# Twelve of sixteen pairs of attention probabilities turned by VectorE blocks and a round trip through HBM instead of by TensorE

## The reference, cut to what matters

```
s = einsum('bnqhgd,bnkhd->bhgnqk', qc, kb) * HEAD_DIM ** -0.5
s = where(valid, s, -1e30)
m = maximum(max(s, -1), sink)
p = exp(s - m)
denom = sum(p, -1) + exp(sink - m)
o = einsum('bhgnqk,bnkhd->bnqhgd', p / denom, vb)
```

## Time and profile before

| what | value |
|---|---|
| time, median of 3 runs | 1270.37 us (1270.3 to 1270.75) |
| profiled execution, its own time | 1270.71 us |
| its span, first to last instruction | 1268.9 us |
| PE, DVE, ACT, POOL busy | 99%, 70%, 49%, 57% |
| mean granted TensorE clock | 0.999 of full speed |
| attention stage, first scores to last values | 818.9 to 969.7 us |
| HBM traffic | 136.20 MB read, 14.16 MB written |

### The profile page before, as it was taken

The page is one execution under the profiler, slowest core; times in us unless marked ns, Lnnn a source line. Parts: engine busy times, 40 slices in busy tenths (PEclk is TensorE's granted clock), DMA queues, the critical chain, the costliest instruction groups (busy, mean ns, idle before and its releaser), DMA issues.

```text
span 1268.9 us, 19753 instructions
## 1 busy us (share of the span) xinstructions
PE 1261.5 (99%) x7542; PEld 1091.2 (86%) x7542; DVE 893.3 (70%) x1380; ACT 619.7 (49%) x989; POOL 724.1 (57%) x513
## 2 busy tenths in 40 slices
PE   9999999999999999999999999999999999999998
PEld 7877877777888899989988998877778899999886
DVE  6775555777444599558855869766656999998587
ACT  6123533565334555325522546354556656666454
POOL 3543433434543588658865866444333786666767
PEclk9999999999999999999999999999999999999999
DMA  7253176564423335353535335333522233225351
GB/s 225 87 150 108 42 199 159 144 187 125 124 75 100 100 100 166 100 166 100 167 101 166 103 106 174 108 88 88 137 67 68 76 121 100 89 83 199 100 210 73
DMA packets 205371, 154.89 MB, mean 122 GB/s; under 512 B 67488, under 2 KB 194976, under 8 KB 204512
## 3 DMA queue, kind: packets, MB, share of 16 engines
q1 hardware_dynamic: 204800, 153.06, 40.3%
q10 hardware_dynamic: 480, 0.59, 0.1%
HBM read 136.20 MB, written 14.16 MB: 118 GB/s over the span
## 4 chain that ended last, share of the span: by engine, by line
PE 96%; ACT 1%; DVE 1%; DMA 1%; POOL 1%; issue 0%; SPq 0%; ACTq 0%
PE gemm L961 16%; PE gemm L962 16%; PE gemm L969 16%; PE gemm L1235 10%; PE gemm L1234 10%; PE gemm L1239 10%; PE gemm L985 2%; PE gemm L986 2%; PE gemm L991 2%; PE gemm L1018 2%; PE gemm L1019 2%; PE gemm L1024 2%; PE mix L1355 1%; PE mix L1343 1%; PE mix L1332 1%; DMA raw<-w_in 1%
## 5 line engine op out<-in xcount | busy, mean ns | idle before, releaser
L793 POOL TENSOR_TENSOR wlo<-raw,whi 128x512 fp32r<-128x512 f32 x264 | 368.7, 1428 | 288.6 <-ACT whi L1491 269.1
L961 PE MATMUL gemm<-hh,whi 128*128 128x512 f32 x544 | 215.3, 396 | 0.2 <-ACT whi L1491 0.2
L962 PE MATMUL gemm<-hl,whi 128*128 128x512 f32 x544 | 212.4, 390 | 0.0
L813 POOL TENSOR_TENSOR wlo<-raw,whi 128x512 fp32r<-128x512 f32 x108 | 159.4, 1501 | 40.5 <-ACT whi L1685 32.4
L1491 ACT ACTIVATE whi<-raw 128x2048 fp32r<-128x2048 f32 x62 | 118.4, 1909 | 46.0 <-PE gemm L969 19.8
L969 PE MATMUL gemm<-hh,wlo 128*128 128x512 f32 x544 | 136.0, 391 | 0.0
L1234 PE MATMUL gemm<-hh,whi 128*128 128x256 f32 x496 | 124.8, 284 | 0.0
L961 PEld LDWEIGHTS gemm<-hh,whi 128*128 128x128 f32 x544 | 102.1, 188 | 26.3 <-issue 4.3
L1235 PE MATMUL gemm<-hl,whi 128*128 128x256 f32 x496 | 124.4, 284 | 0.0
L962 PEld LDWEIGHTS gemm<-hl,whi 128*128 128x128 f32 x544 | 102.3, 188 | 20.4
L969 PEld LDWEIGHTS gemm<-hh,wlo 128*128 128x128 f32 x544 | 101.7, 188 | 20.9
(11 more groups left out here) (545 smaller groups left out, 3124.6 us busy)
## 6 DMA issues: line engine op xcount, KB each, us to landing
raw<-w_in SPq DMA_DIRECT2D x53, 1024.0 KB, 5.3
raw<-w_gu SPq DMA_DIRECT2D x44, 512.0 KB, 5.2
raw<-w_down SPq DMA_DIRECT2D x16, 512.0 KB, 4.4
p_rows<-p_blocks SPq DMA_DIRECT2D x32, 160.0 KB, 3.2
p_t<-p_rows SPq DMA_DIRECT2D x8, 640.0 KB, 4.0
raw<-w_o SPq DMA_DIRECT2D x5, 1024.0 KB, 5.2
raw_b<-w_branch SPq DMA_DIRECT2D x16, 256.0 KB, 6.8
blk_b<-w_o SPq DMA_DIRECT2D x8, 512.0 KB, 7.1
```

The source lines that it names most:

```text
L793: last = nc.gpsimd.tensor_tensor(a(wlo), a(raw), as_f32(a(whi)), ALU.subtract)
L813: return nc.gpsimd.tensor_tensor(part_of(wlo, u, b), raw_block(u, f, k), as_f32(part_of(whi, u, b)), sub)
L961: mm(bank[:, :], w, xh[:, k, :], start=(k == 0), stop=False)
L962: mm(bank[:, :], w, xl[:, k, :], start=False, stop=False)
```

## The change

The first 24 steps (12 pairs, `BY_DMA`) are no longer turned by PE. After `w_norm`, DVE turns every 32x32 block of both steps into `w_blocks` (two buffers of 128x1024). SP stores that with four DMAs of 128 KB in runs of 1 KB to `w_rows`, which puts each block row in its place. ACT waits for the store in slot 2v+3 and issues one DMA of 512 KB back into `w_turned_p` (two buffers). PE takes pair v's values in slot 2v+5, an odd slot of its own, and reads its moving operand as four runs of 32 columns. The last 8 steps keep the old way. SP's order is written out anew, with 12 stores in it. The loads of `lng`, `lnb` and `bsb`, whose room the new buffers take, move from before the stage to behind pair 11's values. In the first block SP now waits for the value product before the store instead of after it.

```diff
+        w_blocks = [place(f"w_blocks{i}", [P, 1024], Z0 + at) for i, at in enumerate((80, 98))]
+        w_turned_p = [place(f"w_turned_p{i}", [P, 1024], Z0 + 68 + 4 * i) for i in range(2)]
+        BY_DMA = 12
+        S_PE = 2 * BY_DMA
...
                 sp.wait_ge(sem("p_turned"), i + 1)
-                for f in range(4):
-                    sp.dma_start(p_rows[i % 2].rearrange("(j a) (k c) -> a k j c", a=32, c=P)[:, :, :, 32 * f:32 * f + 32],
-                                 p_blocks[32 * f:32 * f + 32, :].rearrange("a (k j b) -> a k j b", j=4, b=32)).then_inc(sem("p_stored"), 16)
                 if 2 <= i < HEADS + 2:
                     sp.wait_ge(sem("mo_o"), i - 1)
                 elif i >= HEADS + 2:
                     sp.wait_ge(sem("st_o"), i - HEADS - 1)
+                for f in range(4):
+                    sp.dma_start(p_rows[i % 2].rearrange("(j a) (k c) -> a k j c", a=32, c=P)[:, :, :, 32 * f:32 * f + 32],
+                                 p_blocks[32 * f:32 * f + 32, :].rearrange("a (k j b) -> a k j b", j=4, b=32)).then_inc(sem("p_stored"), 16)
...
+            def store_probs(v):
+                sp.wait_ge(sem("w_tb"), v + 1)
+                if v >= 2:
+                    sp.wait_ge(sem("w_v"), 2 * v - 2)
+                for f in range(4):
+                    sp.dma_start(w_rows[v % 2].rearrange("(j a) c -> a j c", a=32)[:, :, 256 * f:256 * f + 256],
+                                 w_blocks[v % 2][32 * f:32 * f + 32, :].rearrange("a (j c) -> a j c", j=4)).then_inc(probs_stored(v)[0], 16)
...
+            load_qz(n_qz + 6)
+            store_probs(2)
+            store_probs(3)
+            swap_rotary(2)
+            store_turned(2)
+            load_qz(n_qz + 7)
+            store_probs(4)
+            store_turned(3)
             load_wide(0)
+            store_probs(5)
+            store_probs(6)
             swap_rotary(3)
             store_turned(4)
+            load_wide(1)
+            store_probs(7)
...
+            store_probs(10)
+            slot_free(n_ao)
+            load(n_ao, cols(w_ao, 0, UC))
+            store_probs(11)
+            sp.wait_ge(sem("w_v"), S_PE)
+            sp.dma_start(lng[:, :], ln_g.partition_broadcast(P)).then_inc(sem("c2_in"), 16)
+            sp.dma_start(lnb[:, :], ln_b.partition_broadcast(P)).then_inc(sem("c2_in"), 16)
+            sp.dma_start(bsb[:, :, :].rearrange("p g i -> p (g i)"), sg_b.partition_broadcast(P)).then_inc(sem("c2_in"), 16)
             for u in range(1, 4):
+                slot_free(n_ao + u)
+                load(n_ao + u, cols(w_ao, u * UC, UC))
...
             def w_values(s):
                 m, c = s // TT, s % TT
-                pe.wait_ge(sem("w_pt"), s + 1)
+                if s < S_PE:
+                    pe.wait_ge(probs_in(s // 2)[0], probs_in(s // 2)[1] + 16 * (s // 4 + 1))
+                    by_block = w_turned_p[s // 2 % 2].rearrange("p (f k b) -> p k f b", k=8, b=32)
+                    turned = lambda k: by_block[:, s % 2 * 4 + k]
...
             def w_slot():
...
-                    for s in (i - 4, i - 3):
-                        if 0 <= s < STEPS:
-                            w_values(s)
-                if 0 <= i - 2 < STEPS:
+                first = i - 4 if i % 2 == 0 else i - 5
+                if (S_PE <= first < STEPS) if i % 2 == 0 else (0 <= first < S_PE):
+                    w_values(first)
+                    w_values(first + 1)
+                if S_PE <= i - 2 < STEPS:
                     w_turn(i - 2)
...
+            def load_probs(v):
+                act.wait_ge(probs_stored(v)[0], probs_stored(v)[1] + 64 * (v // 2 + 1))
+                act.dma_start(w_turned_p[v % 2][:, :], w_rows[v % 2]).then_inc(probs_in(v)[0], 16)
...
             def w_slot():
...
-                if 0 <= i - 2 < STEPS:
+                if S_PE <= i - 2 < STEPS:
                     w_turned(i - 2)
+                if i % 2 and 3 <= i < S_PE + 3:
+                    load_probs((i - 3) // 2)
...
             def attention_consts():
+                for h in range(2):
+                    v.memset(w_blocks[0].rearrange("p (j k b) -> p k j b", j=4, b=32)[:, 2 * h], 0.0)
...
+            def w_blockwise(v_):
+                dve.wait_ge(sem("w_p"), 2 * v_ + 2)
+                if v_ >= 2:
+                    dve.wait_ge(probs_stored(v_)[0], probs_stored(v_)[1] + 64 * (v_ // 2))
+                blocks = w_blocks[v_ % 2].rearrange("p (j k b) -> p k j b", j=4, b=32)
+                for s in (2 * v_, 2 * v_ + 1):
+                    probs = wp[:, s % 3].rearrange("p h (k j b) -> p (h k) j b", j=4, b=32)
+                    own = blocks[:, s % 2 * 4:s % 2 * 4 + 4]
+                    if s % TT == 0:
+                        for k in (1, 3):
+                            last = v.transpose(own[:, k], probs[:, k])
+                    else:
+                        last = v.transpose(own, probs)
+                last.then_inc(sem("w_tb"), 1)
```

More of the change, by code:

```diff
@@ L322, in build_program, with probs_stored, probs_in @@
         STEPS = KD * TT
+        BY_DMA = 12
+        def probs_stored(v):
+            return (sem("p_stored"), 64 * 2 * HEADS) if v % 2 else (sem("w_stored"), 0)
+        def probs_in(v):
+            return (sem("p_in"), 16 * 2 * HEADS) if v % 2 else (sem("w_in"), 0)
+        S_PE = 2 * BY_DMA
         W_AT = ((12,), (4, 20), (12,), (4, 20))
@@ L370, in build_program @@
         xs_rows = nc.dram_tensor("xs_rows", (SEQ, BW), f32, kind="Internal").ap()
+        w_rows = nc.dram_tensor("w_rows", (2, P, 1024), f32, kind="Internal").ap()
         p_rows = nc.dram_tensor("p_rows", (2, P, 1280), f32, kind="Internal").ap()
@@ L719, in store_turned @@
                                  x_turned[m % 4][32 * f:32 * f + 32, :].rearrange("a (j b) -> a j b", b=32)).then_inc(sem("x_stored"), 16)
[L721 to L734, removed]
@@ L735, in _, with load_qz @@
-            slot_free(n_vs)
+            def store_probs(v):
[5 more added lines that the diff above has]
+                                 w_blocks[v % 2][32 * f:32 * f + 32, :].rearrange("a (j c) -> a j c", j=4)).then_inc(probs_stored(v)[0], 16)
+            def load_qz(n):
+                slot_free(n)
+                p, j = divmod(n - n_qz, 2)
+                load(n, cols(w_in2, (I2_ZA if j else I2_Q) + p * UC, UC))
@@ L736, in load_wide @@
             def load_wide(u):
+                slot_free(n_vs + u)
                 slot = raw[:, (n_vs + u) % 2].rearrange("p (k a) c -> p k (a c)", a=2)
                 load(n_vs + u, cols(w_in2, I2_VS + u // 2 * 512, 512, 4 * (u % 2), 4), slot)
+            load_qz(n_qz)
+            load_qz(n_qz + 1)
+            sp.wait_ge(sem("key_s"), 1)
+            for a, b in ((0, 8), (8, 0)):
+                for kv in range(2):
+                    sp.dma_start(key_t[a:a + 8, kv, :], key_s[64 * kv + b:64 * kv + b + 8, :]).then_inc(sem("key_in"), 16)
@@ new lines, in _ @@
+            load_qz(n_qz + 2)
+            swap_rotary(0)
+            load_qz(n_qz + 3)
+            load_qz(n_qz + 4)
+            store_probs(0)
+            swap_rotary(1)
+            store_turned(0)
+            load_qz(n_qz + 5)
+            store_probs(1)
+            store_turned(1)
+            load_qz(n_qz + 6)
[6 more added lines that the diff above has]
+            store_turned(3)
@@ L740, in _ @@
             load_wide(0)
+            store_probs(5)
+            store_probs(6)
             swap_rotary(3)
             store_turned(4)
+            load_wide(1)
+            store_probs(7)
+            store_turned(5)
+            load_wide(2)
+            store_probs(8)
+            store_turned(6)
+            load_wide(3)
+            store_turned(7)
+            store_probs(9)
+            store_probs(10)
+            slot_free(n_ao)
+            load(n_ao, cols(w_ao, 0, UC))
+            store_probs(11)
@@ L1348, in w_values @@
                 m, c = s // TT, s % TT
-                pe.wait_ge(sem("w_pt"), s + 1)
+                if s < S_PE:
[3 more added lines that the diff above has]
+                else:
+                    pe.wait_ge(sem("w_pt"), s - S_PE + 1)
+                    turned = lambda k: wpt[:, s % 2, k * P:(k + 1) * P]
                 if c == 0 and m >= 1:
@@ L1355, in w_values @@
                         last = mm(M[3][64 * h:64 * h + 64, c * P:(c + 1) * P], v2[:, c - 1 + kb_, kv * DH:(kv + 1) * DH],
-                                  wpt[:, s % 2, (2 * h + kb_) * P:(2 * h + kb_ + 1) * P],
+                                  turned(2 * h + kb_),
                                   start=(kb_ == keys_of(c)[0]), stop=(kb_ == 1))
@@ L1835, in w_exp @@
                     s = 2 * v + e
-                    if s >= 3:
-                        act.wait_ge(sem("w_t"), s - 2)
+                    if s >= S_PE + 3:
+                        act.wait_ge(sem("w_t"), s - 2 - S_PE)
+                    elif s >= 3:
+                        act.wait_ge(sem("w_tb"), (s - 3) // 2 + 1)
                     for h in range(2):
```

21 lines of the change are left out of this document (8 added, 13 removed).

## The result

The changed kernel takes 1275.12 us (median of 6, 1272.73 to 1276.56) against 1270.34: 1.0035 times as long, 95% interval 1.0024 to 1.0047. It is slower by about a third of a per cent, where a gain to 1264.4 had been forecast. The profiled execution took 1272.73 us (span 1270.6), 1.7 us of span more than before.

The account below looks back on a forecast made before the run. PE was taken to bound the kernel, being busy nearly throughout. A gain of 6.6 less 0.5 of stalls gave 6.1 us, so 1264.6 from the profiled 1270.7, named 1264.4 for the median; range 1262.8 to 1270.6.

Parts of the forecast that it names:

- TensorE's account: PE in the attention stage: 9.1 us saved by 84 fewer transposes, less 2.3 and 0.2 for values' new places: 6.6.
- The wait moved in the first block: SP's wait ahead of the first block's store: no cost; without cover, one 3.2 us landing for each of six heads.
- Strided reading: Rival, chance 0.05: PE reading turned rows in four runs of 32 columns costs 6 us, giving 1270.5.
- Does DVE hold?: Attention stage: 15.8 us of block transposes fit DVE's 60 us free; early maxima come 1 to 2 us late.
- The tight place: First wide unit's low parts: margin of 2.4 us becomes -0.3; stall booked 0.3 us, bounds 0 and 1.5.
- The round trip: Store and load of turned pairs: margin 2.5 us in wide units, 5 before; stall booked 0.2, bounds 0 and 1.
- This, not the store: ACT reaching slot 2v+3 at 12.4 us, not the store landed at 11.7, starts a pair's load.
- SP's order: Stores ahead of weight loads in SP, and the wait ahead of the `lng`, `lnb`, `bsb` loads: no cost.

Follow-up runs that it names:

- x-rows-last run: Changed kernel, twelve pairs, blocks behind `att_t`, SP's stores of x rows 4 to 7 moved behind `store_probs(11)`: 1267.11 us (0.9973).
- runs with blocks alone: Kernel before, PE turning everything, plus DVE making blocks of 12 pairs, nothing stored or loaded: 1275.69 us ahead of the gate, 1270.91 behind `att_t`.
- second profile: The changed kernel measured again, unaltered: 1273.88 us (1.0026); its profiled execution took 1274.18 us.
- rotary rows first: Changed kernel with `swap_rotary` 1, 2 and 3 each issued in SP ahead of the store that stood before it: 1280.15 us (1.0075).
- stall injected: Kernel before the change with three more ACT copies ahead of the first wide unit's split: 1277.31 us (1.0050).

## Why the prediction was wrong

- **TensorE's account** (9.1 - 2.3 - 0.2 = 6.6) was right. The x-rows-last run has 5.8 us of offset at 943 us and 0.8 of waits before it. Two pairs gave 1.0 where the text had 1.09. The wait moved in the first block cost nothing, as forecast: the offset is the same at 50 and at 800 us.
- **Strided reading**: no cost, as forecast (1.08 us for a pair's values, 1.07 before).
- **"Does DVE hold?" is the step that failed.** Two errors are in its working: 60 us were called free from busy times, though nearly half of the idle time up to the first wide unit lies inside the pair's own chain; and operations were priced at durations of before, though the blocks move the gate into POOL's low parts, where it takes twice as long. And it left out that a PE that is ahead by its gain leaves DVE that much less time. The maxima of pair 7 came 3.9 us later behind their scores than before, not 0.5. The control for the blocks' place is the pair of runs with blocks alone, 1275.69 ahead of the gate and 1270.91 behind it; in the full change the same move gave 5 to 6 us.
- **The tight place** had been named, with the right chain and a bound of 1.5 us. Counted from pair 7's scores, POOL began at 897.94 - 882.03 = 15.9 us, before at 896.75 - 885.70 = 11.05: 4.9 later, where 1.4 - 0.3 + 0.5 = 1.6 was booked, plus 1.1 for a PE that comes earlier. With PE 0.7 earlier in this stretch, the margin of 2.4 became 2.4 - 4.9 - 0.7 = -3.2, the stall measured.
- **The lowered clock** was in no term: 3.4 us at 1.2 GHz behind the stall, 1.7 us.
- **The round trip** had less margin than computed, by two terms. The first is the store. Its issue and landing were put at 4 us, with 5.6 as the upper bound; from first issue to last landing the twelve stores took 3.6 to 7.4, the median 6.4, and seven of them were over the bound. (The 3.9 us that the page gives is one of the four DMAs from its own issue.) The second is what starts the load: "This, not the store", the text says of ACT's slot at 12.4 us. In all twelve pairs ACT issued the load within 0.1 us of the store's landing, and pairs 8 and 9 waited:

```profile
ACT whi L1547 <- DMA w_rows<-w_blocks: 3.2, 2, 2.8
ACT za_e L1564 <- DMA w_rows<-w_blocks: 1.6, 1, 1.6
```

  Pair 8 is the worst. Its blocks were ready 13.3 us behind its scores (7.7 booked), the store landed at 19.9 and the load at 26.2, taking 6.3 where 4.0 was booked. The other loads took 3.2 to 4.9. The two waits of line 1410 are pairs 8 and 9, 1.1 us together, 2.3 in the second profile; 0.2 had been booked, for pair 10, which had none. The Trainium skill's rule against a plain DMA with a rearranged pattern for a transpose ("DMA: Bandwidth & Descriptors", rules for kernel authors) is not put to the test by any run here: these stores move whole runs of 1 KB, and pair 0's 512 KB took 3.6 us.
- **SP's order**, of which the text says "I cost all this at nothing", is no neutral matter: with the blocks behind `att_t` three orders gave 1267.1, 1269.0 and 1275.0 us, with the blocks ahead two gave 1275.1 and 1280.2.
- **The stage behind** gave up 1.8 us more: I read it as a race of DVE and POOL for the ports, decided by 0.24 us before and 0.04 after. Before, DVE was first:

```profile
1013.67 1.28 DVE L2825 SCALAR_TENSOR_TENSOR vg<-vg,sml,lnb 128x1024 f32<-128x1024 f32 x1
...
1013.91 2.21 POOL L834 TENSOR_TENSOR wlo<-s_u,whi 128x512 fp32r<-128x512 f32 x1 [1.35 <-ACT whi L1717]
```

```profile
1013.80 2.33 DVE L2909 SCALAR_TENSOR_TENSOR vg<-vg,sml,lnb 128x1024 f32<-128x1024 f32 x1
...
1013.76 1.29 POOL L883 TENSOR_TENSOR wlo<-s_u,whi 128x512 fp32r<-128x512 f32 x1 [1.07 <-ACT whi L1773]
```

After, POOL was, and DVE's chain to the sums of the next stage is 1 us longer, twice, which line 1283 pays (offset -0.2 at 943, +0.6 at 1034, +1.6 at 1044). It is the same in every profiled kernel in which twelve pairs go the new way, and absent with six and eight. It is absent too in the three kernels that hold back the loads of `lng`, `lnb` and `bsb` as the change does but leave the turning to PE, so these late loads by themselves are not it. What puts ACT and DVE 0.3 us apart from about 980 us on stays open.

The sum for the profile: -6.6 + 3.2 + 1.7 + 1.1 + 1.8 = +1.2 against a measured +1.7. As this profile lay 0.5 us ahead from its first 20 us on, 1.0 is not accounted for. The median lies another 2.4 over the profile, of which the second profile explains about half by longer waits of the same line.

## What to carry to other kernels

Idle time of an engine counts as room only where it isn't a wait inside the chain that is being delayed: take the waits by releaser, not 100% minus busy. Take off what a faster engine ahead of it will gain. When an edit shifts DVE's operations, look at what GpSimd does at the new time, since operations with two SBUF inputs may double. Price a transfer from its first issue to its last landing, with the weight loads of that place in flight. Put new work behind what others wait for: here that one move was worth 5 to 6 us and turned a loss into a small gain. And try a smaller dose: eight pairs gave as much as twelve in the best order.

## What had not been expected of the hardware

- A stall of 3.2 us of PE was followed by 3.4 us at 1.2 GHz, and one of 1.95 us likewise (blocks behind `att_t`); one of 6.0 us came with 6.8. The length of the stall alone doesn't decide: waits of 2.5 us at 852.8 and 2.3 at 883.7 with the rotary rows first were not followed by any, nor those of up to 1.9 us in the profile with the stall injected.
- An operation of 0.64 us on DVE took 1.25 when it met POOL's, and POOL's group of four 6.89, against 5.0 in its shortest.
- SP's issue of the eight 64 KB DMAs of two x rows took 10.24 us with a wait for landing between them; the four of one x row alone took 1.9 to 3.8. One DMA of 128 KB in runs of 1 KB took 0.44 us to issue in the median and 0.30 to 1.90 at the ends.
